# Scaling the two head groups after the output product, and reordering the router's transposes, in a hybrid attention and expert-choice MoE layer

## The reference, cut to what matters

```python
o = concatenate([rms_norm(oa, out_norm_a), rms_norm(ob, out_norm_b)], axis=-1)
x = x + einsum('bse,ed->bsd', o, w_o)
h2 = rms_norm(x, norm_ffn)
aff = softmax(einsum('nd,de->ne', h2, w_router), axis=-1)
gates, idx = top_k(aff.T, cap)             # each expert its 64 tokens
x = x + sum over experts of gates * SwiGLU(h2[idx])
```

## Time and profile before

| | us |
|---|---|
| three timed runs | 1192.36, 1195.5, 1195.73 |
| their median | 1195.5 |
| the profiled execution | 1190.94 |
| its span in the trace | 1189.1 |
| attention ends, `route` begins | about 450 |
| first output product starts | 463.1 |
| `route` ends (barrier) | 592.4 |
| first expert matmul | 623.1 |

### The profile page before, as it was taken

How to read it: one execution, slowest core, us unless ns; L and a number is a source line. 1 busy time by engine, 2 the same in 40 slices (tenths; PEclk the granted TensorE clock), 3 DMA queues, 4 the chain that set the end, 5 groups by cost and what they waited for, 6 DMA issues and landing times. The chain is left out here.

```text
span 1189.1 us, 16857 instructions
## 1 busy us (share of the span) xinstructions
PE 1076.0 (90%) x5699; PEld 908.9 (76%) x5699; DVE 922.1 (78%) x1244; ACT 771.5 (65%) x1029; POOL 271.8 (23%) x280
## 2 busy tenths in 40 slices
PE   5799988799988995999719999999999999999996
PEld 4699976688777874788607888888888888888885
DVE  5687768899898881335668888998898888889882
ACT  5454438588888871332236777777777787777772
POOL 1365542001126610211150011111110111111111
PEclk9899989899999997999759999999999999999998
DMA  7123040000012005662149899999999999999992
GB/s 278 50 103 133 1 195 1 1 36 19 19 72 72 36 19 214 213 212 107 71 160 336 325 384 390 395 394 406 399 394 394 395 393 392 397 408 395 394 343 35
DMA packets 72654, 266.94 MB, mean 224 GB/s; under 512 B 5976, under 2 KB 8107, under 8 KB 72347
## 3 DMA queue, kind: packets, MB, share of 16 engines
q1 hardware_dynamic: 65274, 240.61, 52.4%
q0 software_dynamic: 7328, 25.68, 7.7%
HBM read 239.53 MB, written 26.74 MB: 224 GB/s over the span
## 5 line engine op out<-in xcount | busy, mean ns | idle before, releaser
L1693 DVE TENSOR_TENSOR lo<-raw,hi 128x2048 fp32r<-128x2048 f32 x189 | 427.9, 2290 | 63.4 <-ACT hi L1628 63.3
L1628 ACT ACTIVATE hi<-raw 128x2048 fp32r<-128x2048 f32 x192 | 364.6, 1918 | 71.9 <-PE ps L1545 65.3
L1543 PE MATMUL ps<-hi,xehi 128*128 128x512 f32 x512 | 202.3, 395 | 3.2 <-DVE xelo L1698 3.2
L1544 PE MATMUL ps<-lo,xehi 128*128 128x512 f32 x512 | 200.5, 392 | 0.0
L1545 PE MATMUL ps<-hi,xelo 128*128 128x512 f32 x512 | 200.3, 391 | 0.0
L1543 PEld LDWEIGHTS ps<-hi,xehi 128*128 128x128 f32 x512 | 96.9, 189 | 23.5 <-issue 2.9
L1545 PEld LDWEIGHTS ps<-hi,xelo 128*128 128x128 f32 x512 | 96.9, 189 | 20.3
L1544 PEld LDWEIGHTS ps<-lo,xehi 128*128 128x128 f32 x512 | 97.0, 190 | 19.6
L1056 ACT ACTIVATE prob<-ps,nmax 128x512 f32<-128x512 f32 x128 | 87.9, 687 | 21.2 <-DVE nmax L1111 18.9
L969 PE MATMUL ps<-ident,prob 128*128 128x128 f32 x512 | 79.7, 279 | 18.7 <-DVE probTlo L1107 18.4
L1483 POOL COPY take<-idxT 128x1 uint32 (+1 forms) x15 | 12.8, 852 | 366.5 <-PE ps L1528 366.5
(11 more groups left out here) (232 smaller groups left out, 2105.3 us busy)
## 6 DMA issues: line engine op xcount, KB each, us to landing
raw<-in_w_gate SPq DMA_DIRECT2D x64, 1024.0 KB, 9.2
raw<-in_w_up SPq DMA_DIRECT2D x64, 1024.0 KB, 9.0
raw<-in_w_down SPq DMA_DIRECT2D x64, 1024.0 KB, 9.3
w_raw<-in_w_in SPq DMA_DIRECT2D x8, 592.0 KB, 11.9
x<-in_x SPq DMA_DIRECT2D x8, 512.0 KB, 4.1
woraw<-in_w_o SPq DMA_DIRECT2D x4, 1024.0 KB, 5.0
o<-attention_out SPq DMA_DIRECT2D x8, 512.0 KB, 3.9
xr<-in_x SPq DMA_DIRECT2D x8, 512.0 KB, 4.7
```

The costliest lines, as they stand in the source:

```text
L1543: pe.matmul(ps[:, dst[n], :], xehi[:, c, :], hi[w][:, cols], start=c == 0, stop=False)
L1544: pe.matmul(ps[:, dst[n], :], xehi[:, c, :], lo[w][:, cols], start=False, stop=False)
L1628: act.activation(hi[s][:], raw[s][:], ACT.Copy).then_inc(hi_done, 1)
L1693: dve.tensor_tensor(lo[s][:], raw[s][:], hi[s][:].bitcast(F32), ALU.subtract).then_inc(lo_done, 1)
```

## The change

- `group_rows` goes. The transposes of `o` wait only for its load, and `o` is transposed unscaled. The product of each head group is an accumulation of its own (banks 2 and 3, and 4 and 5, 24 matmuls each), and DVE makes two scaled additions for each group: `xr = WO[0] * ro_A + xr` when the first group is there, `x1 = WO[1] * ro_B + xr` after the second.
- The transposes of `h2` have one bank (6) for two: its first half goes ahead of the product's fifth block, its second ahead of the seventh, after ACT has copied the first half out.
- `LG` and `AT` share bank 7. On PE, `AT` of tile t-3 comes ahead of the router's product of tile t-2, and that product waits for DVE's copy of `AT` (`at_done`) instead of the exponential. On DVE, the copy comes right behind `otlo`, ahead of `h2`.

```diff
-    OT, WO, HT, LG, AT = (0, 1), banks(2, 2), (4, 5), ps[:, 6, 0:EXPERTS], ps[0:EXPERTS, 7, 0:P]
+    OT, WO, HT, LG, AT = (0, 1), (banks(2, 2), banks(4, 2)), 6, ps[:, 7, 0:EXPERTS], ps[0:EXPERTS, 7, P:2 * P]
 ...
-                def h2_transposes(u):
+                def h2_transposes(u, b):
                     pe.wait_ge(h2_done, u + 1)
-                    if u:
-                        pe.wait_ge(ht_copied, 2 * u)
-                    for b in range(2):
-                        for i in range(4):
 ...
+                    if u or b:
+                        pe.wait_ge(ht_copied, 2 * u + b)
+                    for i in range(4):
 ...
                         if u:
-                            pe.wait_ge(x1_done, 2 * u)
+                            pe.wait_ge(group_added, 2 * u)
                         for c in range(KD):
-                            if c == KD // 2 and t >= 2:
-                                h2_transposes(t - 2)
+                            if c in (KD // 2, KD // 2 + 2) and t >= 2:
+                                h2_transposes(t - 2, (c - KD // 2) // 2)
+                            group = WO[c // (C_K // P)]
+                            if u and c == C_K // P:
+                                pe.wait_ge(x1_done, 2 * u)
 ...
-                        last.then_inc(wo_done, 1)
+                            if c % (C_K // P) == C_K // P - 1:
+                                last.then_inc(wo_done, 1)
                     if t < T:
-                        pe.wait_ge(on_done, 2 * t + 2)
+                        pe.wait_ge(o_loaded[t % 3], 16 * (t // 3 + 1))
 ...
+                    if t >= 3:
+                        u = t - 3
+                        pe.wait_ge(aff_done, u + 1)
+                        pe.transpose(AT, aff, k["ident"][:]).then_inc(at_ready, 1)
                     if 2 <= t <= T + 1:
                         u = t - 2
                         if t > T:
-                            h2_transposes(u)
+                            for b in range(2):
+                                h2_transposes(u, b)
                         if u == 0:
                             pe.wait_ge(small_loaded, 32)
                         else:
-                            pe.wait_ge(lexp_done, u)
+                            pe.wait_ge(at_done, u)
 ...
-                    if t >= 3:
-                        u = t - 3
-                        pe.wait_ge(aff_done, u + 1)
-                        if u:
-                            pe.wait_ge(at_done, u)
-                        pe.transpose(AT, aff, k["ident"][:]).then_inc(at_ready, 1)
 ...
-                group_rows(0)
                 for t in range(T + 3):
                     if 1 <= t <= T:
                         u = t - 1
-                        dve.wait_ge(wo_done, u + 1)
+                        dve.wait_ge(wo_done, 2 * u + 1)
+                        dve.wait_ge(ro_done, u + 1)
 ...
                         for n in range(2):
                             cols = slice(n * BANK, (n + 1) * BANK)
-                            dve.tensor_tensor(x1[u % 2][:, cols], WO[:, cols], xr[u % 3][:, cols], ALU.add).then_inc(x1_done, 1)
+                            dve.scalar_tensor_tensor(out=xr[u % 3][:, cols], in0=WO[0][:, cols], scalar=ro(u)[:, 0:1],
+                                                     in1=xr[u % 3][:, cols], op0=ALU.mult, op1=ALU.add).then_inc(group_added, 1)
+                        dve.wait_ge(wo_done, 2 * u + 2)
+                        for n in range(2):
+                            cols = slice(n * BANK, (n + 1) * BANK)
+                            dve.wait_ge(group_added, 2 * u + n + 1)
+                            dve.scalar_tensor_tensor(out=x1[u % 2][:, cols], in0=WO[1][:, cols], scalar=ro(u)[:, 1:2],
+                                                     in1=xr[u % 3][:, cols], op0=ALU.mult, op1=ALU.add).then_inc(x1_done, 1)
 ...
-                    if t + 1 < T:
-                        group_rows(t + 1)
+                    if t >= 3:
+                        u = t - 3
+                        dve.wait_ge(at_ready, u + 1)
+                        dve.tensor_copy(k["affT"][:, u * P:(u + 1) * P], AT).then_inc(at_done, 1)
 ...
                     if t >= 3:
                         u = t - 3
-                        dve.wait_ge(at_ready, u + 1)
-                        dve.tensor_copy(k["affT"][:, u * P:(u + 1) * P], AT).then_inc(at_done, 1)
                         if u >= TS - 1:
```

More of the change, by code:

```diff
@@ L1195, in route @@
         small_loaded, x1_stored, h2_stored = sem("small_loaded"), [sem("x1_stored0"), sem("x1_stored1")], [sem("h2_stored0"), sem("h2_stored1")]
-        sso_done, ro_done, on_done = sem("sso_done"), sem("ro_done"), sem("on_done")
+        sso_done, ro_done, group_added = sem("sso_done"), sem("ro_done"), sem("group_added")
         ot_ready, othi_done, otlo_done = sem("ot_ready"), sem("othi_done"), sem("otlo_done")
@@ L1250, in _ @@
             def _(pe):
-                def h2_transposes(u):
+                def h2_transposes(u, b):
                     pe.wait_ge(h2_done, u + 1)
-                    if u:
-                        pe.wait_ge(ht_copied, 2 * u)
-                    for b in range(2):
-                        for i in range(4):
-                            c = 4 * b + i
-                            last = pe.transpose(ps[:, HT[b], i * P:(i + 1) * P], h2[u % 2][:, c * P:(c + 1) * P], k["ident"][:])
-                        last.then_inc(ht_ready, 1)
+                    if u or b:
+                        pe.wait_ge(ht_copied, 2 * u + b)
+                    for i in range(4):
+                        c = 4 * b + i
+                        last = pe.transpose(ps[:, HT, i * P:(i + 1) * P], h2[u % 2][:, c * P:(c + 1) * P], k["ident"][:])
+                    last.then_inc(ht_ready, 1)
                 for t in range(T + 3):
@@ L1272, in _ @@
                                     cols = slice(n * BANK, (n + 1) * BANK)
-                                    last = pe.matmul(WO[:, cols], lhs[:, c, :], wo[rhs][:, c, cols],
-                                                     start=(c == 0 and rhs == "hi" and lhs is othi[u % 2]),
-                                                     stop=(c == KD - 1 and lhs is otlo[u % 2]))
-                        last.then_inc(wo_done, 1)
+                                    last = pe.matmul(group[:, cols], lhs[:, c, :], wo[rhs][:, c, cols],
+                                                     start=(c % (C_K // P) == 0 and rhs == "hi" and lhs is othi[u % 2]),
+                                                     stop=(c % (C_K // P) == C_K // P - 1 and lhs is otlo[u % 2]))
+                            if c % (C_K // P) == C_K // P - 1:
+                                last.then_inc(wo_done, 1)
                     if t < T:
-                        pe.wait_ge(on_done, 2 * t + 2)
+                        pe.wait_ge(o_loaded[t % 3], 16 * (t // 3 + 1))
                         if t:
@@ L1292, in _ @@
                         else:
-                            pe.wait_ge(lexp_done, u)
+                            pe.wait_ge(at_done, u)
                         for c in range(KD):
-                            pe.wait_ge(ht_copied, 2 * u + c // 4 + 1)
+                            if c % 4 == 0:
+                                pe.wait_ge(ht_copied, 2 * u + c // 4 + 1)
                             last = pe.matmul(LG, h2T[:, c, :], wr[:, c, :], start=(c == 0), stop=(c == KD - 1))
                         last.then_inc(lg_ready, 1)
-                    if t >= 3:
-                        u = t - 3
-                        pe.wait_ge(aff_done, u + 1)
-                        if u:
-                            pe.wait_ge(at_done, u)
-                        pe.transpose(AT, aff, k["ident"][:]).then_inc(at_ready, 1)
             @block.scalar
@@ L1326, in _ @@
                                 act.wait_ge(lg_ready, u)
-                            act.activation(h2T[:, 4 * b:4 * b + 4, :], ps[:, HT[b], :].rearrange("p (a c) -> p a c", a=4),
+                            act.activation(h2T[:, 4 * b:4 * b + 4, :], ps[:, HT, :].rearrange("p (a c) -> p a c", a=4),
                                            ACT.Copy).then_inc(ht_copied, 1)
@@ L1332, in _ @@
                             if t >= 2 and b == 0:
-                                act.wait_ge(wo_done, t - 1)
+                                act.wait_ge(wo_done, 2 * (t - 1))
                             act.activation(othi[t % 2][:, 4 * b:4 * b + 4, :], ps[:, OT[b], :].rearrange("p (a c) -> p a c", a=4),
```

1 line of the change is left out of this document (added).

## The result

The changed kernel takes 1223.05 us (median of four runs, 1218.44 to 1223.71) against 1195.24 for the kernel before (1192.36 to 1195.73). The ratio is 1.023, 95% interval 1.020 to 1.026. The forecast was 1209 us, its range 1203 to 1218: the direction was right, the size was not.

What follows compares the result with a forecast made beforehand. PE's own work was taken to bound the middle of `route`, with chains at its end; 9.45 + 0.7 + 3.5 + 1.5 = 15.1 us on the executions' average 1193.6 gave 1208.7, forecast 1209 us, range 1203 to 1218.

Steps and rivals of the forecast that it cites:

- PE bounds the middle, and any wait is paid in full: Middle of `route`: PE busy 100.33 of 100.34 us, 14.7 us a tile, so anything making PE wait costs its full time.
- The wait, 1.89 us a tile, 9.45 in all: Tiles 3 to 7: router's product waits for DVE's copy of `AT`, delaying the output product 1.89 us each, 9.45 us.
- The scaled additions: DVE's new additions in `route`, taken as equal to plain ones; 0.1 more each would add 1.0 us in all.
- The split, 0.7: Transposes of `h2` in two halves: one more entry into the product for each of seven tiles, 0.7 us, at most 1.4.
- The clock, 1.5: Middle of `route`: longer stretches without product matmuls lower PE's clock; five tiles give 0 to 7.5 us, one fall taken, 1.5.
- The prediction's own sign of being wrong: Changed trace, between tiles: the forecast is wrong if the clock drops below full more than once or twice.
- Rival (a): Middle of `route`: the clock falls in every tile, 6 us more than the forecast, 1215 us; chance 0.16.
- The removed work gives nothing in the middle, and the start gains nothing: Dropping `group_rows` saves nothing where DVE waits or idles; first product still starts at 463.1, as ACT takes `othi` late.
- the bound of 3.4 for the start: Start of the stage: gain from transposes not waiting for the norm, taken as nothing, bounded at 0 to 3.4 us.
- The end, 3.5: End of `route`: tile 7's router product waits for tile 6's copy behind top-eight rounds; residual to barrier 17.3, 3.5 us more.

Runs made afterwards that it cites:

- The two repairs: Kernel before, ACT copying tile 0's `othi` ahead of tile 1's squares: 1191.37 us; changed kernel with that order, affinity copies moved, free banks at the end: 1188.25 us.

## Why the prediction was wrong, step by step

- **PE bounds the middle, and any wait is paid in full**: right. Intervals of 14.83 became 16.83 by the wait alone, and PE idled 1.90 us ahead of the router's product, released by the copy.
- **The wait, 1.89 us a tile, 9.45 in all**: right in place and number, a little small: 2.0 a tile, 10.0 in all. The scaled additions, taken as equal to the plain ones, took 1.41 for two in place of 1.29, and `otlo` starts at X+1.32 in place of X+1.20.
- **The split, 0.7**: 0.14 a tile (14.83 against 14.69), 1.0 in all.
- **The clock, 1.5**: this is the step that failed. It was put at 1.5 us and measured 14.4, which is 12.9 of the 13.7 us by which the middle and the end together exceed the sum (25.25 + 3.5 against 15.1). Both of its factors were too small. The number of falls was taken as one and was five: the earlier trace rows was read as a stretch of 2.7 us that holds and 4.6 as one that may fall, and "five tiles give 0 to 7.5" was in the text, but the value taken was at the low end. With the wait alone, in the kernel before, it fell in all five tiles too, even with 0.55 us of idle time. The moment at which the clock fell at the end of `route` was read as 581.96; a mean of 0.96 over the slice gives 581.98, which changes nothing. The price of a fall was taken from the start of the stage as 1.5, half of 2.9 us; it was 3.2 in four of the five, since the clock stayed low for 6.8 us (511.7 to 518.5), and the router's product, itself slowed from 1.86 to 3.36 us, lies in that time. Four times 3.2 and once 1.6 are 14.4 us. With them the sum of the middle is 10.0 + 1.0 + 14.4 = 25.4, against 25.25 measured. The sentence that named the stretch as nearer to the case that fell pointed the right way, and the number taken did not follow it. The prediction's own sign of being wrong, a clock that drops more than once or twice between tiles, came true.
- **Rival (a)**, the clock falling in every tile, is what happened; its price, 6 us more than the forecast, was the same 1.5 a fall and so too low as well. It was given a chance of 0.16.
- **The removed work gives nothing in the middle, and the start gains nothing**: right. The transposes of tile 0 started as soon as their load had landed (455.39, 6.0 us after the last attention output, where it was 9.5 before), and ACT still took `othi` behind the squares of tile 1, at 462.95. The two repairs show that this order was what held it: ACT's order alone brings the first product 2.2 us forward (15.0 to 12.8 us after the last attention output), and with it the transposes that don't wait for the norm bring 3.5 more (to 9.3), near the bound of 3.4 for the start.
- **The end, 3.5**: right to 0.1 (17.32 for a forecast of 17.3). But the wait that was named was not alone: with it gone, only 1.9 of the 3.5 came back, since the transposes of tile 7's `h2` come later too.
- **Transposes and the clock**: the Trainium skill ("TensorE: Matmul & The Clock Gate", Part 4) says that transposes don't count as a busy PE, and the prediction took falls in all five tiles, its rival (a) (it says "the second rival"), to be likelier by it. The falls came, but the trace disagrees with the rule: with 17 more transposes of float32 in the wait the clock was 1.00 over all five tiles, in one execution, and without them 0.83 to 0.91.

## What to carry to other kernels

A short wait ahead of small matmuls can cost more through the clock than through itself: here 2.0 us of waiting brought 6.8 us of half clock with it, which cost 3.2 us more. Before adding a wait on a full PE, look in the trace for stretches in which PE does the same, idle time beside the same kind of matmuls, and read whether the clock held there; if no such stretch held, take a fall for every repetition, and price the whole time at half clock, with the narrow matmuls in it. When two tensors are put into one bank, place the reader of the first where its engine is idle anyway, not behind the work that PE is about to wait for.

## What the runs showed of the hardware

- The granted clock fell with PE 100% busy in the trace, when the work was two router products (32 matmuls of 16 columns in the records) between eight transposes and the next product: 0.83 over the first of the five tiles, 0.86 over all. It held with 1.7 us idle a tile when the router's product was elsewhere.
- 17 float32 transposes of 128x128, 2.0 us, in the place of the wait, and the clock was full in five tiles of five (one execution); with eight matmuls of 512 columns it was too.
- Two scaled additions from PSUM (128x512, one number for each row) took 1.41 us, where two plain additions took 1.29; the next instruction started 1.32 behind in place of 1.20. One scaled addition took 746 ns in the median and one plain one 686, whether or not a wait stands between the two. The scaled operation of the attention stage at 684 ns did not show that; its factor is a constant.
- What is still open: why the clock stayed low for 6.8 us in most tiles and 3.5 in others of the same kernel, and why it fell once behind a gap of 1.8 us that it survived in the changed kernel. No run here sets these apart.
